# The order of 24 matmuls inside a block product: two PSUM banks in turn instead of one after the other

## The reference

```
h2 = rms_norm(x, w_norm2)
ff = square(relu(h2 @ w_ff1))      # 1024 -> 4096
x  = x + ff @ w_ff2                # 4096 -> 1024
```

## Time and profile before

| what | value |
|---|---|
| time, median of 3 runs | 2199.43 us (2198.41 to 2199.96) |
| profiled execution: span from its first to its last instruction | 2195.1 us |
| TensorE busy | 2162.7 us, 13406 matmuls |
| weight loads busy | 1939.7 us, 13406 loads |
| VectorE, ScalarE, GpSimd busy | 1545.0, 945.9, 131.6 us |
| matmuls issued by `ff1_product` | 4368 |

### The profile page before, as it was taken

How to read it: one execution, slowest core, us unless ns; L and a number is a source line. 1 busy time by engine, 2 the same in 40 slices (tenths; PEclk the granted TensorE clock), 3 DMA queues, 4 the chain that set the end, 5 groups by cost and what they waited for, 6 DMA issues and landing times.

```text
span 2195.1 us, 34691 instructions
## 1 busy us (share of the span) xinstructions
PE 2162.7 (99%) x13406; PEld 1939.7 (88%) x13406; DVE 1545.0 (70%) x2585; ACT 945.9 (43%) x1994; POOL 131.6 (6%) x227
## 2 busy tenths in 40 slices
PE   7999999999999999999999999999999999999998
PEld 7988778999999988888899877889999998888886
DVE  5326767888787787786862367578878787867767
ACT  5124832555555523233331258234555555223233
POOL 5011011000000000000130100010000000000002
PEclk9999999999999999999999999999999999999999
DMA  6101012345555786636221110223464549846363
GB/s 177 53 26 48 21 49 96 132 158 200 197 188 188 290 301 247 221 124 230 87 74 39 40 34 21 72 102 140 168 216 169 204 181 346 301 167 242 137 216 114
DMA packets 213460, 330.13 MB, mean 150 GB/s; under 512 B 14620, under 2 KB 97856, under 8 KB 213296
## 3 DMA queue, kind: packets, MB, share of 16 engines
q1 hardware_dynamic: 209600, 321.66, 41.2%
q0 software_dynamic: 2832, 3.10, 0.7%
q10 hardware_dynamic: 864, 3.15, 0.4%
HBM read 212.02 MB, written 115.64 MB: 149 GB/s over the span
## 4 chain that ended last, share of the span: by engine, by line
PE 90%; DVE 4%; ACT 2%; issue 2%; DMA 1%; SPq 0%; POOL 0%; ACTq 0%; DVEq 0%; POOLq 0%
PE ps L2106 29%; PE ps L2108 29%; PE ps L2107 29%; PE ps L2162 1%; PE ps L2289 1%; PE ps L2269 1%; DMA ff_ops<-row_op 1%; DVE xn L1400 0%; ACT S L1189 0%; PE ps L2223 0%; DVE w_lo L1381 0%; DMA x<-in_x_prompt 0%; DVE h_all L1406 0%; DMA kc<-in_cache_k 0%; DVE vn L1844 0%
## 5 line engine op out<-in xcount | busy, mean ns | idle before, releaser
L2106 PE MATMUL ps<-h_all,w_hi 128*128 128x288 f32 (+1 forms) x1408 | 440.1, 313 | 0.8 <-DVE q L1687 0.6
L2108 PE MATMUL ps<-h_all,w_lo 128*128 128x288 f32 (+1 forms) x1408 | 438.6, 312 | 0.0
L2107 PE MATMUL ps<-h_all,w_hi 128*128 128x288 f32 (+1 forms) x1408 | 438.1, 311 | 0.0
L2106 PE MATMUL ps<-w_hi,h_all 128*128 128x512 f32 (+1 forms) x720 | 272.7, 379 | 2.0 <-DVE x L1535 0.7
L2106 PEld LDWEIGHTS ps<-h_all,w_hi 128*128 128x128 f32 x1408 | 264.7, 188 | 1.5 <-DVE q L1687 1.1
L2108 PE MATMUL ps<-w_hi,h_all 128*128 128x512 f32 (+1 forms) x720 | 265.8, 369 | 0.0
L2107 PE MATMUL ps<-w_lo,h_all 128*128 128x512 f32 (+1 forms) x720 | 265.3, 369 | 0.0
L2107 PEld LDWEIGHTS ps<-h_all,w_hi 128*128 128x128 f32 x1408 | 264.8, 188 | 0.0
L2108 PEld LDWEIGHTS ps<-h_all,w_lo 128*128 128x128 f32 x1408 | 264.7, 188 | 0.0
L2108 PE MATMUL ps<-w_hi,ring_all 128*128 128x512 f32 x544 | 211.8, 389 | 0.0
L2107 PE MATMUL ps<-w_lo,ring_all 128*128 128x512 f32 x544 | 211.8, 389 | 0.0
(11 more groups left out here) (252 smaller groups left out, 4102.2 us busy)
## 6 DMA issues: line engine op xcount, KB each, us to landing
ff_ops<-row_op SPq DMA_DIRECT2D x128, 512.0 KB, 3.3
w_raw<-in_w_ff SPq DMA_DIRECT2D x128, 256.0 KB, 3.7
ring_all<-ff_ops SPq DMA_DIRECT2D x32, 1024.0 KB, 8.2
ring<-ff_ops SPq DMA_DIRECT2D x32, 1024.0 KB, 8.6
ff_raw<-q SPq DMA_DIRECT2D x96, 256.0 KB, 3.2
b_all<-in_w_ff SPq DMA_DIRECT2D x24, 1024.0 KB, 12.1
w_raw<-in_w_in SPq DMA_DIRECT2D x64, 256.0 KB, 3.6
ring<-ff_raw SPq DMA_DIRECT2D x12, 1024.0 KB, 5.6
```

The costliest lines, as they stand in the source:

```text
L2106: pe.matmul(out, sh, mh, start=first, stop=False)
L2107: pe.matmul(out, sh, ml, start=False, stop=False)
L2108: return pe.matmul(out, sl, mh, start=False, stop=last)
```

## The change

Inside a block product the loops are interchanged. Before, the half `g` was the outer loop: 12 matmuls into the first bank, then 12 into the second. Now the depth piece `k` is outermost, then the three part products, and the half innermost: each stationary block (`wh`, `wh`, `wl` of the depth piece) is named by two matmuls in a row, one for each bank. Within one bank the sequence of the 12 additions is what it was. The waits ahead of the product and the `f_used` behind its last matmul stay where they were.

```diff
                 rows = f_rows[kind]
-                for g in range(2):
-                    cols = slice(g * HG, (g + 1) * HG)
-                    for k in range(4):
-                        w = slice(k * P, (k + 1) * P)
-                        ins = product(ps[:, FBANK[kind] + g, 0:HG], wh[:, slot, w], wl[:, slot, w],
-                                      rows[:, 0, k, cols], rows[:, 1, k, cols], k == 0, k == 3)
+                sides = [(ps[:, FBANK[kind] + g, 0:HG], slice(g * HG, (g + 1) * HG)) for g in range(2)]
+                for k in range(4):
+                    w = slice(k * P, (k + 1) * P)
+                    for still, part, first, last in ((wh, 0, k == 0, False), (wh, 1, False, False), (wl, 0, False, k == 3)):
+                        for bank, cols in sides:
+                            ins = pe.matmul(bank, still[:, slot, w], rows[:, part, k, cols], start=first, stop=last)
                 ins.then_inc(f_used, 1)
```

## The result

The changed kernel takes 2201.75 us, median of 17 runs (2198.48 to 2204.83), the kernel before in the same comparison 2199.00 us (17 runs, 2197.11 to 2200.44). The medians differ by 2.75 us; the ratio is 1.0015 with a 95% interval of 1.0008 to 1.0022, that is 3.3 us (1.8 to 4.8), slower and clear of no change.

A forecast was written before the change was run, and what follows sets the result against it. The prediction took TensorE's matmul spacings to bound the kernel. All terms were 0, so the profiled span stayed 2195.1 us; with 4.3 us to the timed median the forecast was 2199.4 us, range 2195.4 to 2203.4 us.

The forecast's parts named there:

- The bound: Block-product stage of both layers: 580.3 us, 26% of the span, nearly nothing but 4368 matmul spacings of 132.5 ns on TensorE.
- Waits: Head and end of each block product: nobody waits for its middle, no new wait is needed; cost 0.
- Reusing the block: Block products: 4 of 6 steps keep the stationary block, yet each matmul still has its load; taken 0.
- Alternating banks: Block products: 4004 added bank changes cost nothing, as two equal 24.79 us stretches showed; taken 0, bounds -2.0 to +2.0 us.
- The pace within a product: First twelve matmuls 1.58 us, second twelve 1.60 us; alternation leaves the sum alone; taken 0, bounds -3.6 to +3.6 us.
- Rival B: Block products: each of 4004 new bank changes costs 7.5 ns, by accumulator turn-round or operand fetch; +30 us, 2229 us; chance 0.08.
- its own threshold of 1.1: Block products: cost in ns per bank change from which Rival B could be told from no change, 4.4 us / 4004.
- its sign of 133.6: Block products: a spacing over 133.6 ns throughout, or a clock below 1.00, would show Rival B.
- Rival A: Block products: 2912 steps keeping the block while changing bank save up to 12.5 ns each, 36.4 us, to 2163.0 us; chance 0.12.
- C: Block products: same block named twice, yet nothing is loaded less often; time 2199.4 us; chance 0.80 together with the forecast.

The follow-up runs named there:

- experiment 1: Kernel before with only the stationary blocks in the new sequence, banks and moving operands in the old: 2198.44 us, one run, beside 2198.75 us for the kernel before.
- experiment 2: Kernel before with only the banks alternating at every matmul, stationary blocks and moving operands in the old sequence: 2197.66 us, one run, beside 2198.75 us.
- 4: Two kernels timed against the kernel before: only moving operands in the new sequence, 2202.40 us, ratio 1.0014; stationary blocks and banks together, 2198.77 us, ratio 1.0002.
- experiment 13: Changed kernel with three extra matmuls per layer in the second block (144, 144 and 48 columns): 2189.67 us, ratio 0.9963 to the kernel before.

## Why the prediction was wrong

*The bound* was read rightly: the stage is its 4368 spacings, and the time followed them: 20 ns a product over 182 products are 3.6 us, and the timed ratio gives 3.3 (1.8 to 4.8).

*Waits: 0.* Right as far as the profiles show. TensorE's stalls stayed in the first eight products of each layer. Their length differs between executions by up to about a microsecond a layer, with and without the change.

*Reusing the block: 0.* Right, by experiment 1 and by the one load per matmul. The Trainium skill ("TensorE: Matmul & The Clock Gate", step-by-step section of part 2) says that keeping weights lets one load once; in these traces there is a load for each matmul, 13406 and 13406, and the runs show no saving.

*Alternating banks: 0 within 2 us.* Right, by experiments 2 and 4. The pair of stretches in the earlier trace rows had said it without a run.

*The pace within a product: 0, "in the middle, since both halves keep their number of matmuls".* This step failed. It measured +20 ns a product, 3.6 us in all, the +3.6 us that the prediction gave as its far bound. Its tacit premise was that the price hangs on the single matmul, so that interchanging them leaves the sum alone. It hangs on what comes before: half 0 is quick only in a long run. Before, the twelve of half 0 had 1578.4 ns and those of half 1 1601.6; now the product's first and second twelve have 1600 each, nearly the slow half's pace. The row with 1.58 and 1.60 us was the sign that the pace of this stage was not a constant, and the change cut exactly what was different about the quick half, twelve matmuls in one run. For the upper bound the prediction had named a mechanism, the one that came true, and it still put the term in the middle; for the lower bound it had none.

That the time fell inside the range is partly luck. The same order has a pace of 3120 ns a product as well, and where both layers had it, in experiment 13, the time was 2189.67 us, below the range's 2195.4.

*Rival B* had the sign, and one of its two causes, "the fetch of moving operands, which now jumps between the halves with every matmul". Its price of 7.5 ns per change was the widest rounding of a timeline; 20 ns over 22 new changes are 0.9 ns, under its own threshold of 1.1, and the spacing of 133.3 ns stayed under its sign of 133.6. Its other cause, the change of bank, fell with experiment 2. The earlier trace rows could not refute the operand's jump: 384-column matmuls take 173.3 ns in both stretches, whichever third of the rows they read, so there was no quick third to lose.

*Rival A* fell as stated: nothing is saved by keeping a block, with or without a change of bank. *C* had the loads right and the time wrong, since it left the order itself without effect. The time of 3120 ns a product, 60 less than before, exists all the same, in a state that the forecast knew nothing of. So does the spread: the changed kernel's 17 runs lie over 6.4 us, the old one's over 3.3. Whether its fastest run of 2198.48 us had a quick layer was not seen; for the kernel with the moving operands' sequence alone it was seen.

Not settled: why the addresses and the run's length matter, and what holds the two states. The runs show where the pace changes, not what is behind it.

## What to carry to other kernels

When a stage is nothing but matmul spacings, measure the spacing by place within the repeating unit, from starts, before reordering it; where two parts with equal work differ by 1%, ask which neighbour each one needs. A reordering that moves no wait and no byte can still change the pace of every matmul behind it, so time it over many runs and read more than one of its profiles, at both ends of the spread. When something is placed ahead of one large operand, measure the spacing again, or move the other operand by as much.

## What the runs showed of the hardware

- The fixed time over the columns is not one number. 288 columns (120 ns at 2.4 GHz, clock 1.00) came at 130.0, 131.5 (half 0 in a run of twelve), 132.8 (runs of six), 133.3 and 133.5 ns (half 1) from start to start; 512 columns (213.3 ns) at 226.7 or 233.3, as means over 12 or more. The Trainium skill ("TensorE: Matmul & The Clock Gate", section on the back-to-back gap) gives 2.5 ns over the columns for an isolated matmul; here, in a stream with a load for each matmul, it is 10 to 20.
- Moving the activations by 32, 64 or 128 bytes against the weights made the kernel 30 to 32 us slower (2228.3 to 2231.1 us), with 128 bytes some 27 of 31 us by starts in the 512-column matmuls; moving both by 128 bytes changed nothing (2198.12 us).
- The alternating order has at least two lasting states, 3200 and 3120 ns for 24 matmuls, over 83 products with the same instructions. The pace changed behind a stall and behind extra matmuls of 40 and 48 columns; for these two widths it went by the place in a pattern of four spacings.
- Changing the bank with every matmul, and naming the same stationary block two or four times in a row, each measured 0 (3180 ns a product, as before).
